# Running sums in two rounded products, taps dealt out anew, and a rank count from a broadcast column

## The chip, the cores and the metric

One Trainium2 chip, one of its cores. The metric is the device time of one execution in microseconds (us), the median of some runs. The engines are TensorE (PE in the profile; its weight loads are PEld), VectorE (DVE), ScalarE (ACT), GpSimd (POOL) and SyncE (SP), which issues most of the loads.

## What is computed

Two layers over 512 tokens of width 1024, all in float32, and a final norm. Each layer adds three things to the residual stream: a mixer, a cross attention into 256 memory tokens, and a retrieval of single-neuron experts (PEER). The change touches the mixer and the retrieval.

The mixer reads one input projection of the normed stream and has three branches. A is stick-breaking attention, B a causal depthwise convolution of 31 taps over 512 channels followed by a layer norm and a swish, C a gated convolution of 3 taps. The running sum of A is what is changed:

```python
z = einsum("bhqd,bhkd->bhqk", qb, kb) * scale          # 8 heads x 64
mask = s_pos[None, :] < t_pos[:, None]
log_beta = log_sigmoid(z)
log_keep = where(mask, log_beta - z, 0.0)
after = cumsum(log_keep, axis=3, reverse=True) - log_keep
a = where(mask, exp(log_beta + after), 0.0)
out = einsum("bhqk,bhkd->bhqd", a, vb)
```

The retrieval takes for each of 8 heads the 16 best of two lists of 128 scores, adds them pairwise, takes the 16 best sums, and splits the index of each into its two list positions (the rank count), by which the experts are looked up.

## The kernel before

Everything lies transposed: channels in the 128 partitions, tokens in the free dimension. A matrix product in float32 precision is made of three fp32r (rounded) matmuls: high part by high part, high by low, low by high. The helper `linear` (L1253) issues them, 24 for a panel of 128 output channels and 1024 inputs. Weight panels come into a ring of four slots by SyncE; the high part of a panel is rounded by ScalarE (L492) or GpSimd (L404), the low part is the difference, by VectorE (L834, L841) or GpSimd (L406, L412). `split[s]` tells TensorE that slot s is ready, `used[s]` that its product is done.

The order of the work is written out by hand, as one program for each engine, with semaphores between them.

The stage of the eight heads, once per layer. TensorE (L1315 to L1341) does for head hd: four score blocks z (key block sb by the tokens from that block on: 512, 384, 256 and 128 columns, 1280 in all, side by side in three PSUM banks) and the mask (L1321, L1322); front panel 2 hd (24 matmuls) and the first four of the eight chunks of front panel 2 hd + 1 (12); it waits for `sp`; then the running sums (L1331, L1332), which multiply sp by a triangle of minus ones and, for each later key block, by a square of minus ones, onto z itself: ten f32 matmuls; then the other four chunks (12 matmuls), and, when ScalarE has taken the exp, the product with v (L1339).

ScalarE (L560 to L580) does abs, exp and ln on z (L563 to L567), rounds a panel (L492), then exp of the finished z (L570). It reloads its function table between some of them. VectorE (L922 to L941) does sp = max(z, 0) + ln(1 + exp(-|z|)) (L925), the low parts of two front panels (`front_low`, L841), and in between the convolution of branch B, one multiply-add of 512 columns for each tap (`taps`, L898 and L900). There are 4 tiles of 31 taps, 124 in all. Head 0 has none, head hd the taps 0 to 15 (odd hd) or 16 to 30 (even hd) of tile (hd - 1) // 2. `cv` (L891) makes the input of one tile in each of heads 0 to 3; `sc` (L907 to L916) does the short convolution of branch C, tiles 0 to 2 in heads 5 to 7.

Behind the heads TensorE does the front panels 16 to 19 (the third tile of `sc` needs panel 16, the fourth panel 19), the gate panels 0 and 1 (L1350, L1351), waits for `conv_ready` of all four tiles, and sums conv over its channels (the mean, L1354); then gate 2, a branch product, the variance (L1362) and so on. VectorE does the 15 taps left over, the low part of the third short convolution, the fourth short convolution and its low part, and then subtracts the mean (L950). GpSimd meanwhile splits the panels of the gates stage (`cut`, L404 and L406).

The retrieval: VectorE finds the best of each list while TensorE does the query and score products, then `pick` (L1021 to L1066) makes the choice for a block of 128 tokens, in steps k = 0 to 7; k = 2 and 6 hold the rank count (L1053 to L1059). Block 0's first steps lie between the lists; the rest of it and block 1 come behind them, and TensorE needs block 1's result for a transpose (`turn`, L1528). GpSimd makes low parts of expert panels (L412) and starts the gathers at that time.

Of the kernel before, what the change touches and what calls it, by code (L numbers as in the profile page):

```python
# [20 lines left out]
P = 128  # L21
T = 512
D = 1024
KC = D // P
# [4 lines left out]
SB_TILES = 4  # L29
SB_HEADS = 8  # L30
# [66 lines left out]
ZCOLS = sum(ZW)  # L97
CONSTS = ("ident", "ones", "negones", "tri", "iota", "negmask", "steps")

# [10 lines left out]
def build_trunk(nc, xT, memT, par_d, const_d, front_d, gates_d, branch_d, back_d, keys_d, expert_d, up_rows, down_rows, outT):  # L110
# [3 lines left out]
    with ctx:  # L114
# [37 lines left out]

        sp = place("sp", E + 4 * T * 4, [ZCOLS], F32)
        soft = place("soft", E + 16 * T * 4, [ZCOLS], F32)
        mhi = place("mhi", E + 8192, [KC, N_MEM], F32R)
# [46 lines left out]

        const = place("const", region(6 * 512 + 128), [6 * P + 2 * TOPK], F32)
        fifteen = place("fifteen", region(32), [1], U32)
        identb = place("identb", region(256), [P], BF16)
        negmaskb = place("negmaskb", region(256), [P], BF16)
        par = place("par", region(PAR_COLS * 4), [PAR_COLS], F32)
        std = place("std", region(T * 4), [T], F32)
        SQ = region(4 * T * 4)
        sq = place("sq", SQ, [2, T], F32)  # L210
        xf = place("xf", SQ + 2 * T * 4, [2, T], F32)
# [14 lines left out]
        dinds = place("dinds", UP + 4096, [4, TOPK], F32)  # L226
        small = place("small", region(64 * 4), [64], F32)
        assert top[0] <= nc.sbuf_usable_end, (top[0], nc.sbuf_usable_end)
        onehot1 = place("onehot1", SQ, [HROWS, NK], F32)
# [31 lines left out]
        def pc(name, k):  # L261
# [16 lines left out]

        z_done, ln_ready, sp_ready, c_done, a_ready, y_done = (
            sem(n) for n in ("z_done", "ln_ready", "sp_ready", "c_done", "a_ready", "y_done"))  # L280
        yhi_ready, ylo_ready = sem("yhi_ready"), sem("ylo_ready")
# [199 lines left out]
        def _(act):  # L481
# [45 lines left out]
            with act.Fori(0, LAYERS) as L:  # L527
# [32 lines left out]
                for hd in range(SB_HEADS):  # L560
# [5 lines left out]
                    act.drain()  # L566
                    A(soft[:, :], soft[:, :], ACT.Ln, bias=1.0).then_inc(ln_ready, 1)  # L567
                    next_panel(2 * hd)
                    act.wait_ge(c_done, n)
# [251 lines left out]
        def _(dve):  # L821
# [48 lines left out]
            V.memset(base_col, 0.0)  # L870
            V.memset(fifteen[:, :], 15)
            dve.wait_ge(const_loaded, 16)
            V.tensor_copy(identb[:, :], cst("ident")).then_inc(consts_ready, 1)
            V.tensor_copy(negmaskb[:, :], cst("negmask")).then_inc(consts_ready, 1)
            dve.wait_ge(x_loaded, 16)
            dve.nop(nofuse=True)
            with dve.Fori(0, LAYERS) as L:
# [40 lines left out]
                def sc_lo(ct):  # L918
                    dve.wait_ge(shi_ready, L * SB_TILES + ct + 1)
                    TT(blo[:, 8 + ct, :], yt[:, ct % 2, :], bhi[:, 8 + ct, :].bitcast(F32), ALU.subtract).then_inc(slo_ready, 1)  # L920

                for hd in range(SB_HEADS):  # L922

                    dve.wait_ge(ln_ready, L * SB_HEADS + hd + 1)
                    STT(out=sp[:, :], in0=zps[:, 0:ZCOLS], scalar=0.0, in1=soft[:, :], op0=ALU.max, op1=ALU.add).then_inc(sp_ready, 1)  # L925
                    front_low(12 + 2 * hd + 4)
                    if hd == 5:
                        sc(0)
                    if hd >= 1:
                        taps((hd - 1) // 2, *((0, 16) if (hd - 1) % 2 == 0 else (16, CV_TAPS)))  # L930
                    if hd < 4:
                        cv(hd)
                    front_low(12 + 2 * hd + 5)
                    if hd >= 6:
                        sc_lo(hd - 6)
                    if hd >= 6:
                        drain()
                        sc(hd - 5)
                    if hd % 2:
                        dve.wait_ge(yhi_ready, L * SB_TILES + hd // 2 + 1)  # L940
                        TT(blo[:, hd // 2, :], ps[:, 7, :], bhi[:, hd // 2, :].bitcast(F32), ALU.subtract).then_inc(ylo_ready, 1)  # L941
                taps(3, 16, CV_TAPS)
                sc_lo(2)
                drain()
                sc(3)
                sc_lo(3)

                dve.wait_ge(mu_done, L + 1)
# [72 lines left out]
                def pick(t, k):  # L1021
# [30 lines left out]
                    if k % 4 == 2:  # L1052
                        TS(rank[:, 1, two], rank[:, 0, two], 4, None, ALU.logical_shift_right)  # L1053
                        drain()
                        TT(rank[:, 1, two], fifteen[:, :].to_broadcast([P, 2 * TOPK]), rank[:, 1, two], ALU.logical_shift_right)
                        drain()
# [181 lines left out]
        def _(pe):  # L1238
# [44 lines left out]
            with pe.Fori(0, LAYERS) as L:  # L1283
# [31 lines left out]
                for hd in range(SB_HEADS):  # L1315
# [8 lines left out]
                    front(2 * hd)  # L1324
                    front(2 * hd + 1, range(0, 4))

                    pe.wait_ge(sp_ready, L * SB_HEADS + hd + 1)
                    for sb in range(TB - 1, -1, -1):
                        z = zps[:, ZO[sb]:ZO[sb] + ZW[sb]]
                        for sj in range(sb + 1, TB):  # L1330
                            MM(z[:, ZW[sb] - ZW[sj]:], cst("negones"), sp[:, ZO[sj]:ZO[sj] + ZW[sj]], start=False, stop=False, skip_group_check=True)  # L1331
                        ins = MM(z, cst("tri"), sp[:, ZO[sb]:ZO[sb] + ZW[sb]], start=False, stop=True, skip_group_check=True)  # L1332
                    ins.then_inc(c_done, 1)
                    front(2 * hd + 1, range(4, KC))

# [330 lines left out]
```

## Time and profile before

| | us |
|---|---|
| median of 3 runs (4048.27 to 4050.2) | 4048.61 |
| the profiled execution | 4045.75 |
| its span, first to last instruction | 4043.9 |
| TensorE busy | 3956.1 |
| VectorE busy | 2794.0 |
| ScalarE busy | 1744.7 |
| GpSimd busy | 1251.2 |

A row of the profile names line, engine, operation, output and inputs. The busy time of TensorE is an overlap of pipelined matmuls, so its price per matmul is read from the distance between starts or from the chain of waits, which follows the work that ended last back in time. The profiler takes one execution; its own time stands against the median above.

### The profile page before, as it was taken

The numbers are of one execution on the slowest core, as the hardware profiler recorded it, in microseconds if no ns is written. First come the engines' busy times: TensorE is split into PE (matmuls) and PEld (weight loads), VectorE is DVE, ScalarE is ACT, GpSimd is POOL, SyncE is SP. The second block draws the span as 40 slices with busy tenths as digits, with TensorE's granted clock in tenths as the row PEclk, the third lists the DMA queues.
The fourth block names the chain that finished last, engine by engine and source line by source line (L and its number), as shares of the span: only waits on it lengthen the run. The fifth ranks groups of instructions, "written<-read, shape, count | busy, mean of one in ns | idle before, by whom it ended". The sixth has DMA issues, their size and how long they took to land.

```text
span 4043.9 us, 59757 instructions
## 1 busy us (share of the span) xinstructions
PE 3956.1 (98%) x19810; PEld 3394.2 (84%) x19810; DVE 2794.0 (69%) x4503; ACT 1744.7 (43%) x3160; POOL 1251.2 (31%) x826
## 2 busy tenths in 40 slices
PE   8999999998999999999999999999989999999998
PEld 6677887798999998888876778877989999988886
DVE  2684351699887977878737843427997979687886
ACT  3633123235666653343345321323356666433333
POOL 1014563442122432222300155733511224223221
PEclk9999999999999999999999999999999999999999
DMA  3112232246878999999721122312567889999994
GB/s 130 47 63 86 101 105 67 99 137 224 311 276 281 404 370 353 353 355 353 261 70 52 58 99 99 120 58 91 176 234 277 307 288 414 359 353 354 353 355 174
DMA packets 360212, 876.39 MB, mean 217 GB/s; under 512 B 29136, under 2 KB 191184, under 8 KB 353104
## 3 DMA queue, kind: packets, MB, share of 16 engines
q1 hardware_dynamic: 152208, 506.63, 34.8%
q0 software_dynamic: 73728, 268.47, 17.8%
q10 hardware_dynamic: 134080, 99.11, 8.1%
q8 instruction: 70, 1.15, 0.1%
q14 instruction: 126, 1.03, 0.1%
HBM read 772.90 MB, written 101.19 MB: 216 GB/s over the span
## 4 chain that ended last, share of the span: by engine, by line
PE 80%; DVE 12%; DVEq 3%; issue 2%; DMA 1%; ACT 1%; POOL 1%; ACTq 0%; SPq 0%; POOLq 0%
PE ps L1253 42%; PE ps L1575 26%; PE ps L1553 3%; PE ps L1274 1%; DVE ubuf L1110 1%; PE ps L1321 1%; PE ps L1266 1%; DVE acc L1117 1%; DMA raw<-in_experts 1%; PE ps L1339 1%; PE ps L1332 1%; PE ps L1331 1%; DVE rank L1053 1%; DVE lookup L1050 1%; DVEq L1155 1%
## 5 line engine op out<-in xcount | busy, mean ns | idle before, releaser
L1253 PE MATMUL ps<-xhi,whi 128*128 128x384 f32 (+1 forms) x3264 | 1185.1, 363 | 16.4 <-ACT weighted L702 9.2
L1253 PE MATMUL ps<-xhi,wlo 128*128 128x384 f32 (+1 forms) x3264 | 1160.8, 356 | 0.0
L1253 PE MATMUL ps<-xlo,whi 128*128 128x384 f32 (+1 forms) x3264 | 1160.4, 356 | 0.0
L492 ACT ACTIVATE whi<-raw 128x1024 fp32r<-128x1024 f32 x666 | 703.5, 1056 | 673.4 <-PE ps L1575 593.1
L1253 PEld LDWEIGHTS ps<-xhi,whi 128*128 128x128 f32 x3264 | 615.7, 189 | 73.7 <-ACT weighted L702 12.7
L1253 PEld LDWEIGHTS ps<-xlo,whi 128*128 128x128 f32 x3264 | 615.5, 189 | 50.4 <-issue 5.3
L1253 PEld LDWEIGHTS ps<-xhi,wlo 128*128 128x128 f32 x3264 | 614.5, 188 | 48.2
L834 DVE TENSOR_TENSOR wlo<-raw,whi 128x1024 fp32r<-128x1024 f32 x472 | 575.0, 1219 | 56.6 <-ACT whi L492 53.2
L1575 PE MATMUL ps<-whi,el 128*128 128x512 f32 x1536 | 597.6, 389 | 0.0
L1575 PE MATMUL ps<-wlo,eh 128*128 128x512 f32 x1536 | 597.5, 389 | 0.0
L1575 PE MATMUL ps<-whi,eh 128*128 128x512 f32 x1536 | 597.5, 389 | 0.0
L448 POOL DMA_INDIRECT ubuf<-in_up_rows,gidx x256 | 290.0, 1133 | 872.0 <-DVE small L1110 836.0
L456 POOL DMA_INDIRECT vbuf<-in_down_rows,gidx x256 | 295.1, 1153 | 682.6 <-DVE acc L1117 655.1
L412 POOL TENSOR_TENSOR wlo<-raw,whi 128x1024 fp32r<-128x1024 f32 x138 | 334.8, 2435 | 442.3 <-ACT whi L492 442.2
L1575 PEld LDWEIGHTS ps<-whi,eh 128*128 128x128 f32 x1536 | 288.3, 188 | 59.9
L1575 PEld LDWEIGHTS ps<-whi,el 128*128 128x128 f32 x1536 | 288.3, 188 | 59.9
L1575 PEld LDWEIGHTS ps<-wlo,eh 128*128 128x128 f32 x1536 | 288.3, 188 | 59.7
L1117 DVE SCALAR_TENSOR_TENSOR acc<-vbuf,small,acc 128x1024 f32<-128x1024 f32 x256 | 328.8, 1284 | 6.1 <-issue 5.9
L404 POOL CAST whi<-raw 128x1024 fp32r<-128x1024 f32 (+1 forms) x86 | 102.2, 1189 | 718.8 <-PE ps L1253 636.8
L1110 DVE CUSTOM_DVE_ANT_1 ubuf<-ubuf,xtok 128x1024 f32<-128x1024 f32 x256 | 309.7, 1219 | 0.0
L1147 DVE TENSOR_TENSOR onehot<-selT,const 128x1024 f32<-128x1024 f32 x192 | 226.2, 1220 | 60.1 <-ACT selT L711 40.5
L1214 DVE TENSOR_TENSOR el<-weighted,eh 128x768 fp32r<-128x768 f32 x128 | 122.6, 958 | 174.7 <-ACT eh L774 174.7
(220 smaller groups left out, 5059.8 us busy)
## 6 DMA issues: line engine op xcount, KB each, us to landing
raw<-in_experts SPq DMA_DIRECT2D x512, 512.0 KB, 6.3
raw<-in_back SPq DMA_DIRECT2D x112, 512.0 KB, 3.2
gate_table<-gbuf SPq DMA_DIRECT2D x48, 1024.0 KB, 9.0
act_e<-early_gelu ACTq DMA_DIRECT2D x124, 384.0 KB, 8.1
gtile<-gate_table ACTq DMA_DIRECT2D x122, 384.0 KB, 8.5
raw<-in_front SPq DMA_DIRECT2D x64, 512.0 KB, 3.3
raw<-in_gates SPq DMA_DIRECT2D x48, 512.0 KB, 3.3
early_gelu<-weighted SPq DMA_DIRECT2D x124, 192.0 KB, 7.1
```

The lines of the kernel that those rows point to most:

```text
L412: eng.tensor_tensor(wlo[:, a:b], raw[:, a:b], whi[:, a:b].bitcast(F32), ALU.subtract).then_inc(split[s], 1)
L448: eng.indirect_dma_start(ubuf[:, e % GB, :, :].rearrange("p a b -> p (a b)"), None, up_rows, bass.IndirectOffsetOnAxis(ap=gidx[:, e:e + 1] ...
L456: eng.indirect_dma_start(vbuf[:, e % GB, :, :].rearrange("p a b -> p (a b)"), None, down_rows, bass.IndirectOffsetOnAxis(ap=gidx[:, e:e + ...
L492: A(whi[:, SLOT[s]:SLOT[s] + 1024], raw[:, SLOT[s]:SLOT[s] + 1024], ACT.Copy).then_inc(rounded[s], 1)
L834: TT(wlo[:, a:a + 1024], raw[:, a:a + 1024], whi[:, a:a + 1024].bitcast(F32), ALU.subtract).then_inc(split[s], 1)
L1110: V.tensor_tensor_reduce(out=ubuf[:, e % GB, :, :], in0=ubuf[:, e % GB, :, :], in1=xtok, scale=1.0, scalar=0.0, op0=ALU.mult, op1=ALU.add, ...
L1117: STT(out=acc, in0=vbuf[:, e % GB, :, :], scalar=coef_col(e), in1=acc, op0=ALU.mult, op1=ALU.add).then_inc(axpy_done, 1)
L1147: ins = TT(hot[:, at:at + 8, :], selT[:, q, 8 * k:8 * k + 8].unsqueeze(2).to_broadcast([P, 8, NK]), cst("iota").unsqueeze(1).to_broadcast( ...
L1214: TT(el[:, k, :, :], weighted[:, :, :], eh[:, k, :, :].bitcast(F32), ALU.subtract).then_inc(el_ready, 1)
L1253: ins = MM(out, w[:, a:a + P], x[:, c, t0:], start=(i == 0 and n == 0), stop=(i == len(chunks) - 1 and n == 2))
L1553: MM(ps[:, k // 4, (k % 4) * NK:(k % 4 + 1) * NK], onehot2[:, k % HROWS, :], onehot1[:, k % HROWS, :], start=True, stop=True).then_inc(row ...
L1575: ins = MM(ps[:, acc_bank(tb, half), :], x[:, parity, m, w], v[:, a:a + T], start=(first and m == 0 and q == 0), stop=(last and m == 1 and ...
```

## The change

Five things.

1. The ten f32 matmuls of a head's running sums become twenty fp32r ones: sp is split into a rounded high part `sphi` (ScalarE) and a low part `splo` (VectorE, in place of sp), and the triangle and the square of minus ones, which are exact, are made once by VectorE at the start (they are no longer in the constants that are loaded).
2. sp, its high and its low part are done in two pieces: the columns 512 to 1279 (key blocks 1 to 3), then 0 to 511 (block 0).
3. TensorE does six instead of four chunks of the second front panel ahead of the sums, and two behind them.
4. The taps are dealt out anew: heads 0 to 7 do 0, 16, 16, 16, 16, 10, 10 and 10; the 30 left over come behind the fourth short convolution instead of in front of the third's low part.
5. The rank count shifts by a column of fours that is broadcast (a tensor_tensor) instead of by an immediate (a tensor_scalar).

```diff
+SP_PARTS = (slice(ZO[1], ZCOLS), slice(0, ZO[1]))
+TAPS_OF = ((0, 0), (0, 16), (16, 32), (32, 48), (48, 64), (64, 74), (74, 84), (84, 94))
-CONSTS = ("ident", "ones", "negones", "tri", "iota", "negmask", "steps")
+CONSTS = ("ident", "ones", "iota", "negmask", "steps")
...
+                    for k, part in enumerate(SP_PARTS):
+                        act.wait_ge(sp_ready, 2 * n - 1 + k)
+                        A(sphi[:, part], sp[:, part], ACT.Copy).then_inc(sphi_ready, 1)
                     next_panel(2 * hd)
                     act.wait_ge(c_done, n)
                     A(soft[:, :], zps[:, 0:ZCOLS], ACT.Exp).then_inc(a_ready, 1)
...
             dve.wait_ge(const_loaded, 16)
+            TS(negones[:, :], cst("ones"), -1.0, None, ALU.mult)
+            TS(tri[:, :], cst("negmask"), 0.0, -1.0, ALU.is_lt, ALU.mult)
...
+                def some_taps(first, last):
+                    for ct in range(SB_TILES):
+                        lo, hi = max(first - ct * CV_TAPS, 0), min(last - ct * CV_TAPS, CV_TAPS)
+                        if lo < hi:
+                            taps(ct, lo, hi)
+
                 for hd in range(SB_HEADS):
 
                     dve.wait_ge(ln_ready, L * SB_HEADS + hd + 1)
-                    STT(out=sp[:, :], in0=zps[:, 0:ZCOLS], scalar=0.0, in1=soft[:, :], op0=ALU.max, op1=ALU.add).then_inc(sp_ready, 1)
+                    for part in SP_PARTS:
+                        STT(out=sp[:, part], in0=zps[:, part], scalar=0.0, in1=soft[:, part], op0=ALU.max, op1=ALU.add).then_inc(sp_ready, 1)
+                    for k, part in enumerate(SP_PARTS):
+                        dve.wait_ge(sphi_ready, (L * SB_HEADS + hd) * 2 + (k + 1))
+                        TT(splo[:, part], sp[:, part], sphi[:, part].bitcast(F32), ALU.subtract).then_inc(splo_ready, 1)
                     front_low(12 + 2 * hd + 4)
                     if hd == 5:
                         sc(0)
-                    if hd >= 1:
-                        taps((hd - 1) // 2, *((0, 16) if (hd - 1) % 2 == 0 else (16, CV_TAPS)))
+                    some_taps(*TAPS_OF[hd])
                     if hd < 4:
                         cv(hd)
                     front_low(12 + 2 * hd + 5)
...
                     if hd % 2:
                         dve.wait_ge(yhi_ready, L * SB_TILES + hd // 2 + 1)
                         TT(blo[:, hd // 2, :], ps[:, 7, :], bhi[:, hd // 2, :].bitcast(F32), ALU.subtract).then_inc(ylo_ready, 1)
-                taps(3, 16, CV_TAPS)
                 sc_lo(2)
                 drain()
                 sc(3)
                 sc_lo(3)
+                some_taps(TAPS_OF[-1][1], SB_TILES * CV_TAPS)
 
                 dve.wait_ge(mu_done, L + 1)
                 for ct in range(SB_TILES):
...
                     if k % 4 == 2:
-                        TS(rank[:, 1, two], rank[:, 0, two], 4, None, ALU.logical_shift_right)
-                        drain()
-                        TT(rank[:, 1, two], fifteen[:, :].to_broadcast([P, 2 * TOPK]), rank[:, 1, two], ALU.logical_shift_right)
+                        TT(rank[:, 1, two], rank[:, 0, two], four.to_broadcast([P, 2 * TOPK]), ALU.logical_shift_right)
+                        drain()
+                        TT(rank[:, 1, two], fifteen.to_broadcast([P, 2 * TOPK]), rank[:, 1, two], ALU.logical_shift_right)
                         drain()
                         TT(rank[:, 1, two], rank[:, 0, two], rank[:, 1, two], ALU.bitwise_and)
                         drain()
...
                     front(2 * hd)
-                    front(2 * hd + 1, range(0, 4))
-
-                    pe.wait_ge(sp_ready, L * SB_HEADS + hd + 1)
+                    front(2 * hd + 1, range(0, 6))
+
                     for sb in range(TB - 1, -1, -1):
+                        pe.wait_ge(splo_ready, (L * SB_HEADS + hd) * 2 + (1 if sb else 2))
                         z = zps[:, ZO[sb]:ZO[sb] + ZW[sb]]
                         for sj in range(sb + 1, TB):
-                            MM(z[:, ZW[sb] - ZW[sj]:], cst("negones"), sp[:, ZO[sj]:ZO[sj] + ZW[sj]], start=False, stop=False, skip_group_check=True)
-                        ins = MM(z, cst("tri"), sp[:, ZO[sb]:ZO[sb] + ZW[sb]], start=False, stop=True, skip_group_check=True)
+                            for x in (sphi, splo):
+                                MM(z[:, ZW[sb] - ZW[sj]:], negones[:, :], x[:, ZO[sj]:ZO[sj] + ZW[sj]], start=False, stop=False, skip_group_check=True)
+                        for x in (sphi, splo):
+                            ins = MM(z, tri[:, :], x[:, ZO[sb]:ZO[sb] + ZW[sb]], start=False, stop=x is splo, skip_group_check=True)
                     ins.then_inc(c_done, 1)
-                    front(2 * hd + 1, range(4, KC))
+                    front(2 * hd + 1, range(6, KC))
 
                     pe.wait_ge(a_ready, L * SB_HEADS + hd + 1)
                     pe.wait_ge(ylo_ready, L * SB_TILES + tile)
```

## Rows read from the trace of the kernel before

**Rows 1.** The page: shares of the span in the chain that ended last.
```profile
PE 80%; DVE 12%; DVEq 3%; issue 2%; DMA 1%; ACT 1%; POOL 1%; ACTq 0%; SPq 0%; POOLq 0%
```
**Rows 2.** Chain of waits, head 1 of layer 0: start us, us, what.
```profile
123.96 8.25 PE ps L1253 x36
132.21 0.34 PE ps L1332 x2
...
136.66 2.75 PE ps L1253 x12
...
145.30 8.25 PE ps L1253 x36
```
**Rows 3.** Timeline, ScalarE, head 1: start us, us, what, idle before.
```profile
129.21 1.28 ACT L567 ACTIVATE soft<-soft 128x1280 f32<-128x1280 f32 x1
130.39 1.05 ACT L492 ACTIVATE whi<-raw 128x1024 fp32r<-128x1024 f32 x1
...
136.70 1.24 ACT L570 ACTIVATE soft<-ps 128x1280 f32<-128x1280 f32 x1 [3.97 <-PE ps L1332]
```
**Rows 4.** Timeline, VectorE, head 1.
```profile
130.51 1.49 DVE L925 SCALAR_TENSOR_TENSOR sp<-ps,soft 128x1280 f32<-128x1280 f32 x1 [9.59 <-ACT soft L567]
131.92 1.22 DVE L841 TENSOR_TENSOR wlo<-raw,whi 128x1024 fp32r<-128x1024 f32 x1
...
133.87 12.33 DVE L900 SCALAR_TENSOR_TENSOR conv<-upad,par,conv 128x512 f32<-128x512 f32 x15
...
147.85 0.68 DVE L941 TENSOR_TENSOR blo<-ps,bhi 128x512 fp32r<-128x512 f32 x1
```
**Rows 5.** Chain of waits: fp32r of 256 and 384 columns, f32 of 128.
```profile
550.98 11.40 PE ps L1253 x95
...
962.18 8.32 PE ps L1253 x48
970.50 1.78 PE ps L1553 x16
```
**Rows 6.** Behind the heads: chain, then VectorE and GpSimd of the timeline.
```profile
281.02 22.05 PE ps L1253 x96
303.07 3.51 PE ps L1354 x8
...
276.64 3.56 DVE L914 SCALAR_TENSOR_TENSOR sc_o<-cpad,par,sc_o 128x512 f32<-128x512 f32 x2
...
281.65 21.17 DVE L900 SCALAR_TENSOR_TENSOR conv<-upad,par,conv 128x512 f32<-128x512 f32 x15
...
303.59 0.69 DVE L909 TENSOR_TENSOR cpad<-ps,sc_c 128x512 f32<-128x512 f32 x1 [0.16 <-issue]
...
307.99 0.69 DVE L920 TENSOR_TENSOR blo<-yt,bhi 128x512 fp32r<-128x512 f32 x1 [0.70 <-ACT bhi L558]
...
313.57 2.37 POOL L412 TENSOR_TENSOR wlo<-raw,whi 128x1024 fp32r<-128x1024 f32 x1 [15.42 <-ACT whi L492]
```
**Rows 7.** Block 1's transposes; then stretches: busy by engine, clock, DMA share, GB/s.
```profile
949.19 0.90 PE L1528 MATMUL ps<-const,eidx 128*128 128x128 f32 x3 [10.59 <-DVE eidx L1083]
...
948.00:952.00 4.00, 2.57 (x8) 2.17 (x9) 3.06 (x5) 3.97 (x6) 0.00 (x0) 0.50 0.13 27
952.00:956.00 4.00, 4.00 (x20) 4.00 (x20) 3.19 (x3) 1.42 (x5) 0.00 (x0) 0.81 0.96 259
```
**Rows 8.** Group of the shift, then timeline rows of VectorE and GpSimd.
```profile
L1053 DVE TENSOR_SCALAR rank<-rank 128x32 uint32<-128x32 uint32 x32 | 35.0, 1094 | 2.9
...
900.12 6.14 DVE L1053 TENSOR_SCALAR rank<-rank 128x32 uint32<-128x32 uint32 x1
...
899.10 7.11 POOL L412 TENSOR_TENSOR wlo<-raw,whi 128x1024 fp32r<-128x1024 f32 x3
...
333.58 1.50 DVE L975 TENSOR_TENSOR sg_first<-sg_first,sg 128x512 f32<-128x512 f32 x1
...
332.17 5.13 POOL L412 TENSOR_TENSOR wlo<-raw,whi 128x1024 fp32r<-128x1024 f32 x2 [16.23 <-ACT whi L492]
```

More of the change, by code:

```diff
@@ L153, in build_trunk @@
         sp = place("sp", E + 4 * T * 4, [ZCOLS], F32)
+        splo = place("splo", E + 4 * T * 4, [ZCOLS], F32R)
         soft = place("soft", E + 16 * T * 4, [ZCOLS], F32)
@@ L201, in build_trunk @@
         el = place("el", E + 2 * 2 * DT * 4, [2, 2, DT], F32R)
-        const = place("const", region(6 * 512 + 128), [6 * P + 2 * TOPK], F32)
-        fifteen = place("fifteen", region(32), [1], U32)
+        const = place("const", region(4 * 512 + 128), [4 * P + 2 * TOPK], F32)
+        shifts = place("shifts", region(32), [2], U32)
+        four, fifteen = shifts[:, 0:1], shifts[:, 1:2]
         identb = place("identb", region(256), [P], BF16)
@@ L207, in build_trunk @@
         par = place("par", region(PAR_COLS * 4), [PAR_COLS], F32)
-        std = place("std", region(T * 4), [T], F32)
+        STD = region(T * 4)
+        std = place("std", STD, [T], F32)
         SQ = region(4 * T * 4)
+        assert SQ == STD + T * 4
+        sphi = place("sphi", STD, [ZCOLS], F32R)
         sq = place("sq", SQ, [2, T], F32)
@@ L227, in build_trunk @@
         small = place("small", region(64 * 4), [64], F32)
+        negones = place("negones", region(P * 4), [P], F32R)
+        tri = place("tri", region(P * 4), [P], F32R)
         assert top[0] <= nc.sbuf_usable_end, (top[0], nc.sbuf_usable_end)
@@ L277, in build_trunk @@
         qkv_copied, vt_done, vt_copied = sem("qkv_copied"), sem("vt_done"), sem("vt_copied")
-        z_done, ln_ready, sp_ready, c_done, a_ready, y_done = (
-            sem(n) for n in ("z_done", "ln_ready", "sp_ready", "c_done", "a_ready", "y_done"))
+        z_done, ln_ready, sp_ready, sphi_ready, splo_ready, c_done, a_ready, y_done = (
+            sem(n) for n in ("z_done", "ln_ready", "sp_ready", "sphi_ready", "splo_ready", "c_done", "a_ready", "y_done"))
         yhi_ready, ylo_ready = sem("yhi_ready"), sem("ylo_ready")
@@ L870, in _ @@
             V.memset(base_col, 0.0)
-            V.memset(fifteen[:, :], 15)
+            V.memset(four, 4)
+            V.memset(fifteen, 15)
             dve.wait_ge(const_loaded, 16)
+            TS(negones[:, :], cst("ones"), -1.0, None, ALU.mult)
+            TS(tri[:, :], cst("negmask"), 0.0, -1.0, ALU.is_lt, ALU.mult)
             V.tensor_copy(identb[:, :], cst("ident")).then_inc(consts_ready, 1)
@@ L1634 @@
     const = np.concatenate([
-        np.eye(P, dtype=np.float32), np.ones((P, P), np.float32), -np.ones((P, P), np.float32),
-        -low, np.tile(i, (P, 1)), low * np.float32(-1e30),
+        np.eye(P, dtype=np.float32), np.ones((P, P), np.float32), np.tile(i, (P, 1)), low * np.float32(-1e30),
         np.tile(np.float32(ROW_START), (P, 1)), np.tile(i[:TOPK], (P, 1))], axis=1)
```

## The prediction

> **What bounds the kernel now.** I read the page first: TensorE is busy for 98% of the span and holds 80% of the chain that ended last, VectorE 12% [rows 1]. So a change pays where it shortens TensorE's own work or a wait of it. Then the chain of waits over one attention head, for the edited matmuls [rows 2]: 36 matmuls of the front panels (8.25 us), the running sums (132.21 to 136.66, 4.45 us), 12 front matmuls (2.75), then the products with v and the next head's scores, until 145.30. One head is 21.34 us with no gap: TensorE sets the pace. The timeline of ScalarE and VectorE in that head shows how much cover each has [rows 3, 4]. Next, the rows of widths for the price of one matmul [rows 5]; then the stage behind the eighth head, where the taps left over are done [rows 6]; then a place where TensorE sat idle, for what idleness costs in clock [rows 7]; last the rank count [rows 8].
>
> **1. The running sums.** Before: 10 f32 matmuls of 2560 columns in 4.45 us. After: each twice in fp32r, 20 matmuls of 128 (8), 256 (6), 384 (4) and 512 columns (2). Prices: 512 columns 2.75/12 = 0.229, 384 columns 8.32/48 = 0.173, 256 columns 11.40/95 = 0.120 us [rows 2, 5]. No row has fp32r at 128 columns. Its upper bound is the f32 matmul of 128 columns, 1.78/8 = 0.222 [rows 5]; its lower one half of the 256-column price plus the excess of that over streaming, 0.067. I take 0.120, the narrowest fp32r row. Sum 8 x 0.120 + 6 x 0.120 + 4 x 0.173 + 2 x 0.229 = 2.83 us: 1.62 us less per head, 13.0 per layer. At 0.222 it is 3.65 (saves 0.8), at 0.067 2.41 (saves 2.0).
>
> The Trainium skill (TensorE: Matmul & The Clock Gate, LDWEIGHTS) gives a weight load as its columns over 1.2, 107 ns for these 128 columns, whatever streams behind it. By it the eight narrow ones take 0.107 and the sum is 2.73 us instead of 2.83; no row of this trace separates load and stream at this width.
>
> **2. The handshake in front of them.** Head 1: ln ends at 130.49 [rows 3]. VectorE's sp of 1280 columns takes 1.49, so 1.04 ns a column plus 0.16: 0.96 for the first 768, 0.69 for the other 512. First part done at 131.47. ScalarE's copy of 1024 columns takes 1.05 [rows 3], 768 take 0.84: done at 132.35. VectorE's subtraction 0.96: splo's first part stands at 133.35, the second at about 133.95. TensorE now has 42 front matmuls ahead of it: 123.96 + 8.25 + 6 x 0.229 = 133.58. So it arrives level with the first part, and needs the second 1.4 us later: no wait, but no slack either. Behind it only 6 front matmuls (1.37 us) cover ScalarE's exp, which takes 1.24 [rows 3]: just covered. Queued on ScalarE behind the two new copies are a panel's rounding (1.05) and the table load; they end near 135.1, before the sums do (136.4), and the panel they round is used two heads later: nothing waits. Cost 0; each 0.1 us of slip in this handshake would be 0.8 per layer.
>
> **3. VectorE in the heads.** Its first low part starts 1.95 us later after ln than before (133.87 against 131.92, the end of the old sp). In head 1 it used to finish its list at 148.53 [rows 4], 18.04 after ln; the taps are as many there, so now 19.99, against TensorE's new 19.72 per head: 0.27 late, and as TensorE has no slack the next head slips by that. Head 3 has a multiply-add of 0.82 where a first tap of 0.6 was: about 0.5. Heads 2 and 4 recover; heads 5 to 7 have only ten taps, 4 us less. I charge 0.8 per layer. At the lower matmul price TensorE would be quicker and the slip 1.5; at the upper one 0.
>
> **4. The taps left over: the largest term.** 94 of 124 taps are now done within the heads, 109 before, so 30 instead of 15 stay behind, and they are moved behind the fourth short convolution. That one needs the last front panel. TensorE runs 96 matmuls (fronts 18 and 19, gates 0 and 1) from 281.02 to 303.07 and then the mean of conv, which needs every tap [rows 6]. Before, VectorE did its 15 taps (281.65, 21.17 us, slowed by GpSimd) inside exactly this stretch and TensorE did not wait. Now VectorE has nothing but one low part until front 19 is done at 281.02 + 22.05/2 = 292.05. Then the short convolution up to its low part, 4.40 undisturbed (303.59 to 307.99), plus 0.69 for it [rows 6]. GpSimd splits the 1536-column branch panel at that same moment; the pair of multiply-adds in the third convolution took 3.56 instead of 1.6 beside a 1024-column split [rows 6], and here I charge one whole 1536-column subtraction, 1.5 x 2.37 = 3.6. Taps begin at 292.2 + 4.4 + 0.7 + 3.6 = 300.9. Thirty at 12.33/15 = 0.822 [rows 4] are 24.7; GpSimd is idle then, as its next work at 313.57 waits for ScalarE [rows 6], which itself waits for the mean. Conv is ready at 325.6 and TensorE was there at 303.07: a wait of 22.6 us per layer. Without the GpSimd stall 19; with a second one 25. What follows the mean keeps its distances. VectorE's idle ten microseconds before 292 give nothing back.
>
> **5. Clock.** After a wait of 10.59 us the granted clock was 0.50, and 0.81 over the stretch 952 to 956, so full about 953.5: 4.3 us of work at 1.2 instead of 2.4 GHz, 2.15 lost [rows 7]. The new wait is longer and I charge the same 2.15 per layer. Bounds 0 (clock kept) and 4.3 (a recovery twice as long).
>
> **6. The rank count.** The shift by an immediate had 35.0 us in 32 calls, though most take 0.18: the rest is waiting for GpSimd [rows 8]. It started at 900.12 within three GpSimd subtractions (899.10 to 906.21) and ended as the last did. The new form reads two tensors, as the sum at 333.58 did: that took 1.50 instead of 0.69 because of the GpSimd operation running, then went in front of the second one, whose pair lasted 5.13 instead of 4.74 [rows 8]. So the new shift waits for one GpSimd operation only. But two more short operations follow it, and each then meets the next GpSimd subtraction: three short ones against three long ones end where the old one ended, save 0.1 to 0.3 twice. With one GpSimd operation there is no difference. I take 0.4 per layer; bounds 0 and the whole wait (rival C). The Trainium skill (SBUF — State Buffer, Who interferes with whom) says the same against this edit: a vector instruction with two SBUF inputs contends with a GpSimd instruction that reads SBUF. By it the gain stays near the 0.4 above; the sum at 333.58 agrees.
>
> At the start VectorE makes two constants more (about 0.4 us before the first matmul) and the constant load is a third smaller: they cancel within 0.5, taken as 0.
>
> **Sum per layer:** + 22.6 + 2.15 - 13.0 + 0.8 - 0.4 = + 12.15; two layers + 24.3. The profiled execution took 4045.75 us (span 4043.9), so 4070; the median of the runs shown is 4048.61, so **4073 us**.
>
> **Rivals.**
> A. 128 columns in fp32r cost what they cost in f32 (0.222). For: one row at 128 and it is f32; against: fp32r at 256 is far below f32. Per layer 24.75 - 6.6 - 0.4 = 17.7, total 4084.
> B. They stream at full rate (0.067). Then 24.75 - 16.3 + 1.5 - 0.4 = 9.5 per layer, total 4068.
> C. The other side: the new shift never waits for GpSimd, and VectorE comes to the third transposes earlier by the shift's excess, 14.7 us per layer. TensorE waits 10.59 there [rows 7], so 10.6 count and the 2.15 of clock, 12.7 instead of 0.4. For: small operand, that chain is VectorE's. Against: the sum at 333.58. Total 4073 - 24.6 = 4049, no change; with B 4043, faster. It decides from 12.5 us saved per layer.
> D. The handshake slips by about 0.5 us a head over the rows: + 8, 4081. For: no slack; against: each link has a row.
>
> **How the numbers follow.** Forecast 45% (own range 4066 to 4079), A 25%, B 12%, C 8%, D 10%. The range 4062 to 4089 leaves out C, the least of B, and A with a long wait. 0.2% is 8.1 us, about what a measurement of this kernel can tell: faster than that needs C with B, 3%; within it C, or a wait near 15 us, 7%; slower 90%.
>
> **What would show it.** In the changed profile: TensorE waits for a VectorE conv tap ahead of the mean, 20 to 25 us, twice; 30 taps in one run behind the short convolution, near 0.82 each; granted clock 0.5 after that; a head of about 19.7 us; splo arriving within 0.3 us of the sums; the three short rank operations together as long as before. It would be wrong if the taps ended before the gates did, if a head took over 20.3 us, or if the wait at the transposes went.

## The result and the profile after

| | before | after |
|---|---|---|
| median, us (4 runs each) | 4048.79 (4048.27 to 4050.2) | 4078.41 (4073.65 to 4081.58) |
| the profiled execution, us | 4045.75 | 4081.58 |
| its span | 4043.9 | 4079.8 |
| TensorE busy | 3956.1 | 3943.6 |
| VectorE busy | 2794.0 | 2812.5 |

The ratio is 1.007, 95% interval 1.0058 to 1.0082: slower, 29.6 us by the medians; forecast were 24.3. The profiled execution is the slowest of its four and stands 35.8 us above the profiled one of before, so the traces show somewhat more than the medians do.

TensorE is busy for 12.5 us less and the kernel is slower: the time is in waits. On the page after, the shares of the chain that ended last, as [rows 1]:

```profile
PE 78%; DVE 13%; DMA 3%; DVEq 2%; issue 2%; ACT 2%; POOL 0%; ACTq 0%; SPq 0%; POOLq 0%
```

The two points more of DMA are loads of expert weights, in a stage that the change does not touch. From the transposes of block 1 [rows 7] to the next layer's heads it lasts 1157.5 us here and 1153.4 before; in layer 0 of the twelve profiled executions below it is 1153.4 to 1157.8.

The chain of waits over head 1 of layer 0 (start us, us, what), as [rows 2]. The sums are L1356 and L1358 now, and 42 front matmuls stand ahead of them:

```profile
122.67 9.62 PE ps L1277 x42
132.29 0.26 PE ps L1358 x2
132.54 0.23 PE ps L1356 x2
...
134.63 0.51 PE ps L1358 x2
135.14 1.38 PE ps L1277 x6
...
142.41 0.75 PE ps L1277 x3
```

The sums last from 132.29 to 135.14, 2.85 us instead of 4.45, and the head 19.74 (122.67 to 142.41) instead of 21.34.

Behind the heads, the chain of waits, as the first part of [rows 6]; L915 are taps, L924 to L931 the fourth short convolution, L1380 the mean:

```profile
269.08 11.19 PE ps L1277 x48
280.36 0.69 DVE cpad L924
...
289.12 0.75 DVE conv L915
289.95 0.75 DVE conv L915
...
313.08 0.76 DVE conv L915
313.89 6.43 PE ps L1380 x8
320.32 8.20 PE ps L1277 x36
```

The timeline there, of VectorE, then of TensorE (last bracket: idle time before, and who ended it):

```profile
280.36 0.69 DVE L924 TENSOR_TENSOR cpad<-ps,sc_c 128x512 f32<-128x512 f32 x1 [9.94 <-PE ps L1277]
...
282.21 4.67 DVE L929 SCALAR_TENSOR_TENSOR sc_o<-cpad,par,sc_o 128x512 f32<-128x512 f32 x2
...
289.12 24.71 DVE L915 SCALAR_TENSOR_TENSOR conv<-upad,par,conv 128x512 f32<-128x512 f32 x30
...
313.89 6.43 PE L1380 MATMUL ps<-conv,const 128*128 128x512 f32 x8 [22.75 <-DVE conv L915]
```

VectorE is idle for 9.94 us, does the fourth short convolution, and then 30 taps. TensorE waits for them for 22.75 us. Where the mean starts, the stretches read (us, busy by engine, granted clock, DMA share, GB/s):

```profile
312.00:316.00 4.00, 2.11 (x3) 1.08 (x4) 1.69 (x3) 0.00 (x0) 0.00 (x0) 0.50 0.00 0
316.00:320.00 4.00, 4.00 (x7) 1.62 (x6) 0.00 (x0) 0.00 (x0) 0.00 (x0) 0.57 0.00 0
320.00:324.00 4.00, 4.00 (x18) 3.17 (x17) 2.49 (x4) 2.88 (x4) 0.00 (x0) 1.00 0.00 0
```

So the lower level, 1.2 GHz, holds behind the wait until about 319.5.

### The profile page after: what moved, and what is told of

Read it like the earlier page. It is cut to its first block, busy times and chain, and to the rows that moved or that the text cites. A ratio compares the mean times of both kernels' runs of the same rounds, so it can differ in the third digit from the quotient of the medians.

```text
span 4079.8 us, 59920 instructions
## 1 busy us (share of the span) xinstructions
PE 3943.6 (97%) x19810; PEld 3393.5 (83%) x19810; DVE 2812.5 (69%) x4554; ACT 1765.6 (43%) x3192; POOL 1249.0 (31%) x826
## 3 DMA queue, kind: packets, MB, share of 16 engines
q8 instruction: 70, 1.15, 0.1%
## 4 chain that ended last, share of the span: by engine, by line
PE 78%; DVE 13%; DMA 3%; DVEq 2%; issue 2%; ACT 2%; POOL 0%; ACTq 0%; SPq 0%; POOLq 0%
PE ps L1277 41%; PE ps L1601 26%; PE ps L1579 3%; DMA raw<-in_experts 2%; DVE conv L915 1%; PE ps L1298 1%; PE ps L1290 1%; PE ps L1345 1%; PE ps L1365 1%; DVE ubuf L1134 1%; DVE rank L1077 1%; DVE acc L1141 1%; DVE lookup L1074 1%; PE ps L1446 1%; PE ps L1464 1%
## 5 line engine op out<-in xcount | busy, mean ns | idle before, releaser
L1277 PE MATMUL ps<-xhi,whi 128*128 128x384 f32 (+1 forms) x3264 | 1181.9, 362 | 19.0 <-ACT weighted L714 11.9
```

Of the source, the lines that this page charges most:

```text
L1277: ins = MM(out, w[:, a:a + P], x[:, c, t0:], start=(i == 0 and n == 0), stop=(i == len(chunks) - 1 and n == 2))
```

## The experiments

Lengths below are distances between the starts of TensorE's first or last instructions of a kind, read from each trace to about 0.1 us, layer 0 / layer 1. "Heads" is from the first score matmul of head 0 to the last product with v of head 7; "to the mean" from there to the first mean matmul; "mean to variance" between their first matmuls.

| kernel | heads | to the mean | mean to variance | median us |
|---|---|---|---|---|
| before | 170.2 / 170.1 | 33.7 / 33.8 | 11.7 / 11.7 | 4048.8 |
| after | 159.5 / 162.4 | 56.7 / 56.6 | 14.5 / 13.9 | 4078.4 |
| 1 taps only | 170.2 / 170.2 | 56.6 / 56.6 | 13.3 / 14.6 | 4099.1 |
| 2 old taps | 166.9 / 166.8 | 37.4 / 37.4 | 11.6 / 11.7 | 4045.9 |
| 3 rank count only | 171.6 / 170.2 | 33.8 / 33.7 | 11.7 / 11.7 | 4049.5 |
| 4 left-over taps first | 158.0 / 158.0 | 46.4 / 46.5 | 14.1 / 14.1 | 4056.6 |
| 5 ten taps in head 0 | 158.2 / 160.9 | 38.3 / 38.3 | 14.2 / 13.2 | 4040.1 |
| 6 taps dealt by slack | 158.5 / 160.8 | 34.0 / 34.1 | 11.7 / 11.8 | 4028.6 |
| 7 six and two chunks | 171.4 / 174.4 | 33.8 / 33.8 | 11.7 / 11.7 | 4051.7 |
| 8 left-over taps left out | 163.6 / 166.7 | 33.8 / 33.8 | 11.6 / 11.6 | 4030.6 |
| 9 dealing of 6, f32 sums | 173.2 / 170.1 | 33.7 / 33.8 | 11.8 / 11.7 | 4051.4 |
| 10 dealing of 6, four and four | 167.7 / 164.8 | 34.1 / 34.0 | 11.7 / 11.8 | 4038.5 |

From the variance to the transposes of block 1 (the prediction's third transposes, [rows 7]) all take 634.1 to 635.6. The kernel before ran beside each group of runs: 4048.24 us beside runs 1 to 4, 4049.94 beside 5 to 8, 4048.12 beside 9 and 10; the ratios are against these.

### 1. The taps alone

The kernel before, with the new dealing (`TAPS_OF` and `some_taps` as in the change) and the new place:

```diff
+                    some_taps(*TAPS_OF[hd])
-                    if hd >= 1:
-                        taps((hd - 1) // 2, *((0, 16) if (hd - 1) % 2 == 0 else (16, CV_TAPS)))
...
-                taps(3, 16, CV_TAPS)
                 sc_lo(2)
                 drain()
                 sc(3)
                 sc_lo(3)
+                some_taps(TAPS_OF[-1][1], SB_TILES * CV_TAPS)
```

> The kernel before with the new dealing and place of the taps alone (running sums in f32, old rank count). Theory T (the loss is the 30 taps behind the fourth short convolution): TensorE waits 23 us ahead of the mean and loses 2.8 us of clock behind it in each layer, the heads stay at 21.3 us as VectorE has slack there: 2 x 25.7 = +51, about 4100 us. Rival R (the loss of the changed kernel comes with the split of the sums, the taps are covered): within 10 us of before.

Measured: 4099.11 us, ratio 1.0126 (1.0111 to 1.0142). The wait ahead of the mean is there whole, with the old sums:

```profile
325.88 4.40 PE L1360 MATMUL ps<-conv,const 128*128 128x512 f32 x6 [22.71 <-DVE conv L901]
```

So the cost comes from the dealing and the place of the taps, not from the sums.

### 2. The new sums with the old taps

```diff
-TAPS_OF = ((0, 0), (0, 16), (16, 32), (32, 48), (48, 64), (64, 74), (74, 84), (84, 94))
+TAPS_OF = ((0, 0), (0, 16), (16, 31), (31, 47), (47, 62), (62, 78), (78, 93), (93, 109))
...
+                some_taps(TAPS_OF[-1][1], SB_TILES * CV_TAPS)
                 sc_lo(2)
                 drain()
                 sc(3)
                 sc_lo(3)
-                some_taps(TAPS_OF[-1][1], SB_TILES * CV_TAPS)
```

> The changed kernel with the old dealing and place of the taps (109 in the heads, 15 ahead of the third low part). Theory T: no wait ahead of the mean; the heads save 1.6 us each on TensorE (13 per layer), but VectorE is 3 us late in heads 5 and 6 and 0.8 in heads 1 and 3 (7 per layer): -6 per layer, less 2 to 4 us in all for stretches at 1.2 GHz inside the heads, about 4040 us (4034 to 4046). Rival R: at or above 4060. A third view (VectorE's slips do not add up, since each is absorbed by the next head): 4028.

Measured: 4045.88 us, ratio 0.9989 (0.998 to 0.9999), at the upper end of what was expected. The heads save 3.3 us instead of 12: VectorE's list is the pace there. In layer 0 TensorE waits 1.79 us for `splo` in head 6 and 3.96 us for the second short convolution in head 7; in layer 1 it waits 0.17 and 3.93 us there, and a stretch at the lower clock in head 6 takes the rest: the heads are as long. What the expectation lacked is the third short convolution, which the 16 taps in head 7 push back to 273.51; TensorE's front panel 18 waits for it:

```profile
279.16 0.50 PE L1277 MATMUL ps<-xhi,whi 128*128 128x512 f32 x1 [2.53 <-DVE yt L931]
```

Heads plus way to the mean are 204.3 us, against 203.9 before. The matmuls' 13 us are not seen at all while VectorE has the same taps to do.

### 3. The rank count alone

The column of fours is made at the start, as in the change.

```diff
-                        TS(rank[:, 1, two], rank[:, 0, two], 4, None, ALU.logical_shift_right)
+                        TT(rank[:, 1, two], rank[:, 0, two], four.to_broadcast([P, 2 * TOPK]), ALU.logical_shift_right)
```

> The kernel before with the rank count's new form alone. Theory T: the first short operation waits for one GpSimd subtraction, each of the next two for one more, so that the three end where they did: 0 to -1 us, 4048 us, and the wait of TensorE at block 1's transposes stays near 10.6 us. Rival C (the new form does not wait for GpSimd): -20 to -25 us, 4025, that wait gone.

Measured: 4049.53 us, ratio 0.9999 (0.999 to 1.0008). Rival C is refuted: TensorE still waits 9.25 and 10.33 us at the transposes of block 1. But the mechanism is not the one that step 6 gave. The timeline of VectorE in this kernel, to be read against [rows 8]:

```profile
900.65 6.38 DVE L1055 TENSOR_TENSOR rank<-rank,shifts 128x32 uint32<-128x32 uint32 x1
907.11 0.19 DVE L1057 TENSOR_TENSOR rank<-shifts,rank 128x32 uint32<-128x32 uint32 x1
...
918.50 2.58 DVE L1055 TENSOR_TENSOR rank<-rank,shifts 128x32 uint32<-128x32 uint32 x1
921.15 2.33 DVE L1057 TENSOR_TENSOR rank<-shifts,rank 128x32 uint32<-128x32 uint32 x1
```

Once the two-tensor form was held to the end of a train of three GpSimd subtractions, as the immediate form had been (6.14); once it and the operation behind it were held for one at a time. Layer 1 of this kernel has 6.18 and 4.93 us at the same places, the changed kernel 6.51, 4.46, 6.30 and 4.94. So of eight such places one alone shows it held for a single subtraction. Its 32 calls took 36.2 us there, against 35.0 [rows 8].

### 4. The left-over taps first

The changed kernel, with its 30 left-over taps ahead of the third low part, where the 15 had been:

```diff
+                some_taps(TAPS_OF[-1][1], SB_TILES * CV_TAPS)
                 sc_lo(2)
                 drain()
                 sc(3)
                 sc_lo(3)
-                some_taps(TAPS_OF[-1][1], SB_TILES * CV_TAPS)
```

> The changed kernel with its own dealing, but the 30 taps left over ahead of the third low part and the fourth short convolution, where the old 15 stood. Theory T: 15 of them take 21 us beside GpSimd's splits, the others 0.82 each, so conv is ready 12 us after TensorE came, against 23: 10.7 us less per layer, then the mean's subtraction is up to 2 us late as the short convolution comes behind: 4078 - 19 = about 4059 us (4055 to 4064). Rival (the place does not matter, VectorE's total work behind the heads sets the end): within 5 us of the changed kernel.

Measured: 4056.6 us, ratio 1.002 (1.0011 to 1.003). VectorE's taps, then TensorE's wait:

```profile
269.07 32.72 DVE L915 SCALAR_TENSOR_TENSOR conv<-upad,par,conv 128x512 f32<-128x512 f32 x29
...
303.01 2.93 PE L1380 MATMUL ps<-conv,const 128*128 128x512 f32 x3 [12.53 <-DVE conv L915]
```

The place alone costs 10.2 us a layer (22.75 against 12.53). Started at 269 the taps cost more each, 29 in 32.72 us instead of 23.9, as GpSimd is splitting gate panels; but they lose no ten idle microseconds. This trace has no stretch of lower clock in its heads, and they are 158.0 us: the forecast's 13.0 less 0.8.

### 5. Ten taps in head 0

In run 4's trace VectorE is idle for 8.52 us in head 0, behind its last low part. Kernel 4, with ten of the left-over taps put there:

```diff
-TAPS_OF = ((0, 0), (0, 16), (16, 32), (32, 48), (48, 64), (64, 74), (74, 84), (84, 94))
+TAPS_OF = ((0, 10), (10, 26), (26, 42), (42, 58), (58, 74), (74, 84), (84, 94), (94, 104))
...
-                    some_taps(*TAPS_OF[hd])
+                    if hd:
+                        some_taps(*TAPS_OF[hd])
...
                     front_low(12 + 2 * hd + 5)
+                    if hd == 0:
+                        some_taps(0, TAPS_OF[0][1])
```

> The changed kernel with its left-over taps ahead of the third low part (as in the run of 4056.6 us), and with 10 of them moved into head 0 of each layer, behind its second low part of a front panel, where VectorE is idle for 8.5 us (119.98 to 128.59 us of that run's trace). 20 taps are left over instead of 30. Theory V (VectorE's list from head 0 to the mean of the convolution sets the end of that stage, and only what fills an idle stretch of it shortens it): head 0 keeps its length, the wait ahead of the mean falls by 10 x 0.82 = 8.2 us per layer, from 12.5 to about 4.3: 4056.6 - 16.4 = 4040 us, with up to 4 less from the clock after a shorter wait: 4034 to 4044. Rival W (the taps in head 0 delay the next head's low parts, and TensorE, which has no slack, gives the gain back in the heads): the wait shrinks but a head grows by some us; 4048 to 4057.

Measured: 4040.06 us (4038.14 to 4045.62), ratio 0.9979 (0.9969 to 0.999). Layer 0's heads keep their length (layer 1's have stretches of low clock at 2180 and 2220 us), and the wait is the 4.3 us expected:

```profile
294.27 6.21 PE L1383 MATMUL ps<-conv,const 128*128 128x512 f32 x8 [4.29 <-DVE conv L915]
```

### 6. Taps dealt by VectorE's slack

Kernel 5 with five more taps in heads 4 to 7:

```diff
-TAPS_OF = ((0, 10), (10, 26), (26, 42), (42, 58), (58, 74), (74, 84), (84, 94), (94, 104))
+TAPS_OF = ((0, 10), (10, 26), (26, 42), (42, 58), (58, 75), (75, 86), (86, 97), (97, 109))
```

> As the run with 10 taps in head 0, and the heads 4 to 7 get 17, 11, 11 and 12 taps instead of 16, 10, 10 and 10, as far as VectorE's list ends before TensorE's head of 19.74 us does. 15 taps are left over, as in the kernel before. Theory V: the wait ahead of the mean goes to nearly nothing (12.5 - 15 x 0.82 = 0.2), heads stay at 158 to 160 us; per layer the sums' 12.2 us are kept whole: 4048.6 - 24.4 = 4024, and up to 8 more for the stretches of lower clock seen in kernels with the new sums: 4028 us, 4023 to 4036. Faster than both kernels. Rival W: 4040 or more, with heads of 162 us or longer. Rival K (the clock takes back what the matmuls give): heads short, but a mean granted clock below 0.990 and a time above 4036.

Measured: 4028.58 us (4025.59 to 4035.09), ratio 0.9951 (0.9937 to 0.9964): faster than both kernels, by 21.4 and 49.8 us. VectorE in head 0 and the wait ahead of the mean:

```profile
120.66 7.37 DVE L915 SCALAR_TENSOR_TENSOR conv<-upad,par,conv 128x512 f32<-128x512 f32 x9
128.45 1.55 DVE L947 SCALAR_TENSOR_TENSOR sp<-ps,soft 128x768 f32<-128x768 f32 x2 [0.42 <-ACT soft L576]
...
290.91 3.70 PE L1383 MATMUL ps<-conv,const 128*128 128x512 f32 x8 [0.16 <-DVE conv L915]
```

Theory V holds; the mean granted clock is 0.993 in the profiled execution.

### 7. Six and two chunks, f32 sums

```diff
-                    front(2 * hd + 1, range(0, 4))
+                    front(2 * hd + 1, range(0, 6))
...
-                    front(2 * hd + 1, range(4, KC))
+                    front(2 * hd + 1, range(6, KC))
```

> The kernel before, with six instead of four chunks of the second front panel ahead of the running sums and two behind them, as in the changed kernel; the sums stay f32. It tells whether the stretches of granted clock near 0.55 in busy heads, seen in the kernels with the new sums and hardly in those without, come from the order of the matmuls. Theory N (they come with the two-product sums, which are many narrow matmuls): heads keep 170.2 us, save 0.1 to 0.3 a head if ScalarE's exp (1.24 us) is not covered by 1.37 us of matmuls: 4048 to 4052, mean granted clock 0.993 to 0.994. Rival O (order): the same low stretches, mean granted clock near 0.991, 4052 to 4058.

Measured: 4051.74 us (4046.4 to 4053.5), ratio 1.0002 (0.9993 to 1.0011), clock 0.992 to 0.994. The order alone does nothing that can be measured. But its profiled execution has low stretches in its heads too (171.4 and 174.4 us instead of 170.2), so they don't come with the new sums alone: theory N had the time right, but not this.

### 8. The left-over taps left out

```diff
-                some_taps(TAPS_OF[-1][1], SB_TILES * CV_TAPS)
+                some_taps(SB_TILES * CV_TAPS - 1, SB_TILES * CV_TAPS)
```

> The changed kernel with 29 of the 30 left-over taps left out in each layer (the last two tiles of the convolution lack them), so that nothing but one tap stands between the short convolution's low part and the mean. It measures the tail's price by itself. Forecast's terms: the wait of 22.9 us and the clock after it go: 4078.4 - 2 x (22.9 + 2.2) = 4028 us, 4022 to 4034; the distance from the last product with v to the mean goes back to about 34 us. Rival S (the wait is set by the short convolution, which also comes late at about 289 us, and not by the taps): TensorE still waits some us ahead of the mean, 4040 or more.

Measured: 4030.57 us (4029.05 to 4037.1), ratio 0.9951 (0.9936 to 0.9966). The chain around the mean has no wait, so rival S is refuted:

```profile
273.06 22.05 PE ps L1277 x96
295.12 3.43 PE ps L1380 x8
```

So 29 taps are 47.8 us of the kernel (4078.41 - 4030.57), 23.9 a layer: the 22.75 of the wait, and 1.15 of the 2.5 us by which mean to variance had grown. The rest may be hidden by low clock in the heads, which this run's profiled execution has more of than any other (163.6 and 166.7 us); that is not shown. What is left against before, some 18 to 20 us, is the gain of the sums after what the clock takes back.

### 9. The dealing of run 6 with the old sums

The kernel before, with the table and the place of taps of run 6.

> The kernel before with the dealing of the run of 4028.6 us alone (10 taps in head 0, then 16, 16, 16, 17, 11, 11, 12, and 15 left over ahead of the third low part); the sums stay f32. Theory T (TensorE sets the pace of the heads and VectorE's list had just fitted, so that less VectorE work in them is worth nothing by itself): heads 170.2 us, 33.8 to the mean, 4046 to 4052, no change. Rival U (the dealing alone gave that run its gain, for instance because head 0's idle time was on the path): 4040 or less.

Measured: 4051.4 us (4045.46 to 4054.16), ratio 1.0004 (0.9994 to 1.0013). Each half by itself gives next to nothing against the kernel before that ran beside it: the sums with the old taps 2.4 us, the dealing with the old sums nothing, both together 21.4.

### 10. Four and four chunks with the new sums

Run 6 with the chunks as they were before.

```diff
-                    front(2 * hd + 1, range(0, 6))
+                    front(2 * hd + 1, range(0, 4))
...
-                    front(2 * hd + 1, range(6, KC))
+                    front(2 * hd + 1, range(4, KC))
```

> The kernel of the run of 4028.6 us with four instead of six chunks of the second front panel ahead of the running sums and four behind them. It tests the step that said TensorE arrives level with the low part of sp. Theory H (the handshake of sp, high part, low part has no slack): TensorE is at the sums 6 x 0.229 = 1.37 us earlier and waits for it, 1.2 to 1.4 us in each head, twice eight heads: +20 us, 4048 us, 4043 to 4055, with an idle stretch ahead of the first sum in each head that ends with splo. Rival L (there was slack in it): 4036 or less. Rival M (the short waits also lower the clock): above 4055.

Measured: 4038.51 us (4036.72 to 4043.31), ratio 0.9976 (0.9967 to 0.9986): 9.9 us above run 6, half of theory H. TensorE's wait in head 1, then ScalarE's abs and exp in heads 5 and 6 (the timeline):

```profile
131.83 0.33 PE L1361 MATMUL ps<-sphi,tri 128*128 128x128 f32 x1 [1.19 <-DVE splo L950]
...
206.84 1.24 ACT L572 ACTIVATE soft<-ps 128x1280 f32<-128x1280 f32 x1 [4.42 <-PE ps L1349]
208.15 1.27 ACT L574 ACTIVATE soft<-soft 128x1280 f32<-128x1280 f32 x1
...
227.97 1.24 ACT L572 ACTIVATE soft<-ps 128x1280 f32<-128x1280 f32 x1 [2.98 <-PE ps L1349]
229.28 1.28 ACT L574 ACTIVATE soft<-soft 128x1280 f32<-128x1280 f32 x1
```

The wait stands in heads 1 to 4 of layer 0 and 0, 1, 3 and 4 of layer 1, 1.17 to 1.19 us each. The two other heads among the first five have a stretch of low clock instead, in which TensorE comes later by itself and does not wait. From head 5 on, with no sigmoid of `cv` in between, ScalarE still has exp's table, loads none between L572 and L574, and ln comes 1.28 us earlier. Starts of sp are 21.08 us apart in the first heads and 19.8 between heads 5, 6 and 7 of layer 1. Five waits of 1.19 in two layers would be 11.9 us, against the 9.9 measured; the eight that the trace has are 9.5. In the first five heads the handshake had 1.37 - 1.19 = 0.2 us of slack.

## Why the prediction was right

The forecast, 4073 us, rested on two large terms, the shorter sums and the wait for the left-over taps, and both came as it had them.

**Step 1, the sums:** forecast 2.83 us a head, measured 2.85 in head 1. The 128-column fp32r matmul was the term without a row. In run 10's timeline, whose sums start as those of the changed kernel do, it reads:

```profile
132.00 0.28 PE L1361 MATMUL ps<-splo,tri 128*128 128x128 f32 x1
132.11 0.27 PE L1359 MATMUL ps<-sphi,negones 128*128 128x128 f32 x1
132.22 0.28 PE L1359 MATMUL ps<-splo,negones 128*128 128x128 f32 x1
...
132.85 0.22 PE L1359 MATMUL ps<-sphi,negones 128*128 128x128 f32 x1
132.91 0.28 PE L1359 MATMUL ps<-splo,negones 128*128 128x128 f32 x1
...
134.18 0.44 PE L1361 MATMUL ps<-sphi,tri 128*128 128x512 f32 x1
134.46 0.39 PE L1361 MATMUL ps<-splo,tri 128*128 128x512 f32 x1
134.69 0.39 PE L1280 MATMUL ps<-xhi,whi 128*128 128x512 f32 x1
```

From a 128-column matmul to the next start it is 0.11 us, and 0.06 for the two that come straight behind a 256-column one. Neither rival A (0.222) nor rival B (0.067 for all) holds. The Trainium skill (TensorE: Matmul & The Clock Gate, LDWEIGHTS) has 0.107 us for such a weight load; the distances of 0.11 agree, the two of 0.06 lie below it.

That the total came so close is in part luck, as two errors cancelled. In the changed kernel's head 1 the eight narrow matmuls took 0.83 us, not 0.96, and the twelve wider ones 2.02, not 1.87. The excess of these sits at one place: behind the first matmul by the triangle of each key block the next starts 0.03 to 0.06 us later than its width has elsewhere (0.28 instead of 0.23 at 512 columns, above). No run tells why.

**Steps 2 and 3, handshake and VectorE:** forecast no wait and 0.8 us of slip. In a trace without low clock in its heads (run 4) they save 12.2 us of the 13.0. The agreement with 0.8 is half luck: heads 2 and 4 take 19.87 and 20.06 us instead of 19.74, a slip of 0.45 where the step had 0.27 and 0.5; the rest is that the heads save 1.57 to 1.60 us each and not 1.62. Starts of sp lie 19.88 us apart from head 1 to head 2 of the changed kernel; forecast was 19.99. Rival D, half a microsecond a head, did not come. Run 10 shows that "level with the first part" was right for heads 0 to 4, within 0.2 us, and that heads 5 to 7 have 1.28 us more.

**Step 4, the wait:** forecast 22.6 (19 to 25), measured 22.75 at the mean. (Its own rows, 325.6 less 303.07, give 22.5.) Its parts stand too: taps begin 8.85 us behind the last front panel (280.27 to 289.12; forecast 8.85). Beside GpSimd's split of the 1536-column panel the pair of multiply-adds takes 4.67 instead of 1.58 and the multiply ahead of it 0.98 instead of 0.49, 3.6 us together, as charged. And 30 taps take 24.71 (forecast 24.7). The two layers' wait and the clock behind it are the whole difference between a loss and a gain (run 8).

**Step 5, clock:** forecast 2.15 a layer, bounds 0 and 4.3; mean to variance grew by 2.8 and 2.2.

**Step 6, rank count:** the size was right (0.4 forecast; no change in run 3), the mechanism was not. "The new shift waits for one GpSimd operation only" failed: it was held for 6.38 us in run 3, to the end of the train, and for a single subtraction in one place of eight. The row at 333.58 on which the step leaned [rows 8] showed the rarer outcome. What carried the forecast was its other half: whatever the first operation escapes, the next one meets (2.58, then 2.33 us).

**What the sum lacked.** The terms as measured give -12.2 + 22.75 + 2.5 = 13.05 a layer, 26 in all. The medians differ by 29.6, the two profiled executions by 35.8. Of the 9.7 us between 26 and 35.8, 5.9 are stretches of lower clock in busy heads, which no step had: the heads took 159.5 and 162.4 us instead of 158.0. Another 4.1 lie in the stage behind the transposes of block 1 in layer 0 (1157.5 against 1153.4 us), which the change does not touch; the rest, 1.3 us less ahead of the first head and about 1 more elsewhere, nearly cancels. One of the stretches, with TensorE busy throughout, and TensorE's timeline there:

```profile
2180.00:2182.00 2.00, 2.00 (x7) 0.64 (x6) 1.85 (x3) 0.14 (x1) 0.00 (x0) 1.00 0.00 0
2182.00:2186.00 4.00, 4.00 (x13) 2.90 (x14) 3.63 (x6) 2.56 (x3) 0.00 (x0) 0.64 0.00 0
...
2179.64 1.12 PE L1345 MATMUL ps<-qT,kT 64*128 64x512 f32 x2
...
2182.64 0.48 PE L1345 MATMUL ps<-qT,kT 64*128 64x128 f32 x2
2183.06 0.28 PE L1346 MATMUL ps<-negmaskb,identb 128*128 128x128 bf16 x1
2183.09 0.78 PE L1277 MATMUL ps<-xhi,whi 128*128 128x512 f32 x1
```

It costs 4 x (1 - 0.64) = 1.4 us in these four. The place is nearly always the same. The profiled executions of the twelve kernels have 32 stretches of low clock in their heads. Two follow a wait (run 2, head 7), two begin early in head 0, and the other 28 all begin 3.2 to 3.6 us after a head's first score product, where the scores end. In 24 of them TensorE has just done, without a pause, some 5.3 us of products with v and of scores, which use 64 columns or 64 rows, as here; the four in head 0 stand behind a wait of 1.0 us and the scores. Runs of one kernel differ in how many they have: the 27 executions of the kernel before that stood beside runs 1 to 4 go from 4045.28 us at a mean clock of 0.995 to 4055.62 at 0.992. That they come oftener with the new sums is likely but not shown. The five profiled executions with f32 sums have 0, 0, 1, 2 and 3 of them in the heads, the seven with the new ones 0, 2, 2, 4, 4, 5 and 9; over all executions the mean clock is 0.992 to 0.995 before, 0.990 to 0.993 in run 2 (whose waits explain some of it) and 0.991 to 0.995 in run 6. Why such a place loses the clock in one head and not in the next was not settled.

## What to carry to other kernels

TensorE's saving is worth only what VectorE can follow: from head 0 to the mean, kernels 2 and 4 needed 204.3 and 204.4 us, hardly other than before (203.9), whichever way the same taps were dealt behind head 0. What turned 12 us of shorter matmuls into time was the idle time of VectorE inside the heads: ten taps in head 0 brought layer 0 to 196.5 us, and five more in heads 4 to 7 to 192.5. When an edit shortens the engine that sets the pace, lay out the second engine's whole list against the new period, head by head, and look for its idle stretches ahead of the work as well as behind it. Work that is queued behind a wait (here for the last front panel) pays for all the idle time of that wait: the place cost 10.2 us a layer (22.75 less 12.53), the smaller number of taps in the heads the other 12.5 (run 4's wait, against 0.16 in run 6).

## What was not expected of the hardware

- The granted clock fell to the lower level for some microseconds in heads where TensorE had not paused at all (0.64 over 2182 to 2186), in some executions and not in others, and in 28 of 32 cases right at the end of a head's score products.
- A 32-column VectorE operation on two tensors, issued while GpSimd subtracts 1024 columns time after time, was held to the end of the train (6.38 us with all three ahead of it, 4.46 to 4.94 with two), and in one place of eight for one at a time (2.58 and 2.33).
- With exp's table still loaded, ScalarE's abs between two exps took no table load: it came 1.28 us earlier to ln, more than the 1.19 us that TensorE waited in the heads with the load (run 10).
